# Router features taken from the unscaled residual and computed inside the output projection of a hybrid delta-net / attention / MoE layer

## What is computed

```python
x = x + merged @ w_out                        # output projection and residual
h = rms_norm(x, norm_ffn_w)                   # x / sqrt(mean(x^2) + eps) * norm_ffn_w
grp_prob  = softmax(h @ w_router_group + b_router_group)        # 4 groups
exp_logits = h @ w_router_expert + b_router_expert              # 16 experts
# best group, the best two experts in it, their weights; each chosen expert:
#   silu(h @ w_gate) * (h @ w_up) @ w_down, weighted and added to x
return rms_norm(x, norm_final_w)
```

## Time and profile before

| | |
|---|---|
| median of 3 runs | 768.96 us (768.24 to 773.33) |
| profiled execution, own time | 771.36 us |
| its span | 769.6 us |
| PE busy | 674.8 us (88%) |
| DVE / ACT / POOL busy | 62% / 50% / 22% |
| mean granted PE clock | 0.926 |

### The profile page before, as it was taken

The page is one execution under the profiler, slowest core; times in us unless marked ns, Lnnn a source line. Parts: engine busy times, 40 slices in busy tenths (PEclk is TensorE's granted clock), DMA queues, the critical chain, the costliest instruction groups (busy, mean ns, idle before and its releaser), DMA issues.

```text
span 769.6 us, 9253 instructions
## 1 busy us (share of the span) xinstructions
PE 674.8 (88%) x3386; PEld 557.1 (72%) x3388; DVE 479.9 (62%) x789; ACT 383.1 (50%) x647; POOL 169.5 (22%) x216
## 2 busy tenths in 40 slices
PE   5998796968989999999698999989999999999820
PEld 4677675746768888888587788658878888888710
DVE  5686646455452233444267265579989999999527
ACT  7366532523342243323343125237888988998612
POOL 6000000069700000000000000014555555555200
PEclk9999997978798999999899998689999999999965
DMA  8513311240032211112213735056877877977144
GB/s 263 183 56 62 58 45 56 69 137 1 5 84 85 61 55 56 55 55 94 72 55 110 282 155 199 22 157 192 282 220 232 287 241 249 317 252 254 39 153 191
DMA packets 73712, 104.62 MB, mean 136 GB/s; under 512 B 31625, under 2 KB 53186, under 8 KB 73538
## 3 DMA queue, kind: packets, MB, share of 16 engines
q1 hardware_dynamic: 60912, 95.57, 38.4%
q0 software_dynamic: 12672, 8.43, 3.6%
q10 hardware_dynamic: 82, 0.03, 0.0%
HBM read 123.89 MB, written 17.83 MB: 184 GB/s over the span
## 4 chain that ended last, share of the span: by engine, by line
PE 78%; DVE 9%; ACT 6%; issue 4%; DMA 3%; SPq 1%; DVEq 0%; ACTq 0%; POOLq 0%
PE bank L1510 20%; PE bank L1512 19%; PE bank L1511 19%; PE bank L1894 2%; PE bank L1639 2%; PE bank L1853 2%; PE bank L1837 2%; DMA w_raw<-in_w_in 1%; ACT w_hi L706 1%; ACT square_kq_T L740 1%; PE bank L1670 1%; PE bank L1657 1%; DMA expert_rows<-expert_rows_hbm 1%; DVE down_lo L1294 1%; PE bank L1669 1%
## 5 line engine op out<-in xcount | busy, mean ns | idle before, releaser
L1510 PE MATMUL bank<-h_hi,w_hi 128*128 128x512 f32 x304 | 125.3, 412 | 3.3 <-DVE h_lo L995 2.4
L1511 PE MATMUL bank<-h_lo,w_hi 128*128 128x512 f32 x304 | 120.3, 396 | 0.0
L1512 PE MATMUL bank<-h_hi,w_lo 128*128 128x512 f32 x304 | 120.2, 395 | 0.0
L1294 DVE TENSOR_TENSOR gate_up_lo<-ew_raw,gate_up_hi 128x1024 fp32r<-128x1024 f32 x92 | 108.3, 1220 | 6.0 <-ACT gate_up_hi L901 3.6
L653 POOL DMA_INDIRECT unit_tokens<-ffn_rows,row_index x23 | 30.8, 1338 | 320.3 <-DVE row_index L1416 304.7
L978 DVE TENSOR_TENSOR w_lo<-w_raw,w_hi 128x2048 fp32r<-128x2048 f32 x26 | 59.8, 2299 | 64.2 <-ACT w_hi L706 64.2
L901 ACT ACTIVATE gate_up_hi<-ew_raw 128x1024 fp32r<-128x1024 f32 x92 | 92.1, 1056 | 9.9 <-DMA ew_raw<-in_w_gate,extra_weight_rows 8.3
L1510 PE MATMUL bank<-gate_up_hi,unit_in_hi 128*128 128x512 f32 x184 | 75.8, 412 | 0.0
L1512 PE MATMUL bank<-gate_up_hi,unit_in_lo 128*128 128x512 f32 x184 | 72.2, 392 | 0.0
L1511 PE MATMUL bank<-gate_up_lo,unit_in_hi 128*128 128x512 f32 x184 | 71.8, 390 | 0.0
L1510 PEld LDWEIGHTS bank<-h_hi,w_hi 128*128 128x128 f32 x304 | 58.5, 192 | 14.8 <-DVE w_lo L990 2.6
(11 more groups left out here) (353 smaller groups left out, 1334.4 us busy)
## 6 DMA issues: line engine op xcount, KB each, us to landing
w_raw<-in_w_in SPq DMA_DIRECT2D x17, 1024.0 KB, 5.2
ew_raw<-in_w_gate SPq DMA_DIRECT2D x32, 512.0 KB
ew_raw<-in_w_up SPq DMA_DIRECT2D x32, 512.0 KB
ew_raw<-in_w_down SPq DMA_DIRECT2D x32, 512.0 KB
w_raw<-in_w_out SPq DMA_DIRECT2D x4, 1024.0 KB, 5.1
expert_rows<-expert_rows_hbm SPq DMA_DIRECT2D x8, 512.0 KB, 6.6
x_T<-in_x SPq DMA_DIRECT2D x4, 512.0 KB, 5.3
w_raw<-in_w_in SPq DMA_DIRECT2D x8, 256.0 KB, 4.3
```

The source lines that it names most:

```text
L1294: dve.tensor_tensor(dst, eraw[slot][:, :], hi.bitcast(F32), ALU.subtract).then_inc(elo_done, 1)
L1510: pe.matmul(out_ap, lhs_hi, rhs_hi, start=first, stop=False)
L1511: pe.matmul(out_ap, lhs_hi, rhs_lo, start=False, stop=False)
L1512: return pe.matmul(out_ap, lhs_lo, rhs_hi, start=False, stop=last)
```

## The change

The router no longer reads the normed tokens. PE transposes the residual y itself, in natural feature order, 4 blocks at a time: `residual_turn(0, t)` after each tile of the third quarter of the output projection, `residual_logits(0, t)`, `residual_turn(1, t - 1)` and `residual_logits(1, t - 2)` after the tiles of the fourth. What is left over follows the projection. The turns go round banks 4, 5 and 6, all logits are summed in bank 7. ACT copies the first halves of all tiles, DVE the second halves. norm_ffn_w is loaded as 8 more columns of `small_cols` and multiplied into the router weights once; the two router weight loads move in SP's queue from the start to the side projection, with another layout. DVE multiplies the logits by the norm's factor while adding the bias (4 instructions for 1). ACT's square sums come after its four copies and write to another scratch place. `ffn_norm(3)` moves behind the choice of experts on DVE. The fill matmuls are as before.

```diff
-        rows = at("small_rows", [57, P], F32, r_tmp + 4096)
+        rows = at("small_rows", [65, P], F32, r_tmp + 4096)
-        hf = at("ffn_in_F", [P, KT, S], F32, r_h + 16384)
+        hf = [at(f"residual_F{i}", [P, 4, S], F32, o) for i, o in enumerate((r_o, r_b + 8192))]
+        junk_m = at("square_junk_ffn", [P, D], F32, ffn_raw + 8192)
...
+                if u == U_SIDE + 4:
+                    sp.dma_start(rw_raw[:, :, 0:NG], a["w_router_group"][0].rearrange("(k p) n -> p k n", k=KT)).then_inc(x2_in, 16)
+                    sp.dma_start(rw_raw[:, :, NG:], a["w_router_expert"][0].rearrange("(k p) n -> p k n", k=KT)).then_inc(x2_in, 16)
-                    sp.dma_start(rw_raw[:, :, 0:NG], a["w_router_group"][0].rearrange("(p k) n -> p k n", k=KT)).then_inc(small_in, 16)
-                    sp.dma_start(rw_raw[:, :, NG:], a["w_router_expert"][0].rearrange("(p k) n -> p k n", k=KT)).then_inc(small_in, 16)
...
+            act.dma_start(rows[57:65, :], a["norm_ffn_w"][0].rearrange("(k p) -> k p", p=P)).then_inc(rows_in, 16)
...
             for t in range(TT):
+                act.wait_ge(tt_ps, t + 1)
+                act.activation(hf[0][:, :, t * P:(t + 1) * P], bank4(4 + t % 3), ACT.Copy).then_inc(hf_act, 1)
+            act.wait_ge(lo_done, split_count(UNITS_PRE - 1))
+            for t in range(TT):
                 act.wait_ge(y_done, 4 + t + 1)
                 if t:
                     act.wait_ge(ssq2, t)
-                act.activation(junk[:, :], y[:, t, :], ACT.Square, accum_out=ssq[:, t:t + 1]).then_inc(ssq2, 1)
+                act.activation(junk_m[:, :], y[:, t, :], ACT.Square, accum_out=ssq[:, t:t + 1]).then_inc(ssq2, 1)
...
-            for t in range(TT):
-                act.wait_ge(tt_ps, t + 1)
-                act.activation(hf[:, 0:4, t * P:(t + 1) * P], bank4(4 + 2 * (t % 2)), ACT.Copy).then_inc(hf_act, 1)
...
-            dve.wait_ge(x2_in, 48)
+            dve.wait_ge(x2_in, 80)
+            dve.tensor_tensor(rw_raw[:, :, :], rw_raw[:, :, :], bc_last(cols[:, 57:65], NG + NE), ALU.mult)
...
+            def residual_features(t):
+
+                dve.wait_ge(tt_ps, TT + t + 1)
+                dve.tensor_copy(hf[1][:, :, t * P:(t + 1) * P], bank4(4 + (TT + t) % 3)).then_inc(hf_dve, 1)
 
             for t in range(TT):
                 residual(0, t)
             residual(1, 0)
-            residual(1, 1)
-            ffn_norm(0)
-            residual(1, 2)
-            ffn_norm(1)
-            residual(1, 3)
-            ffn_norm(2)
-            ffn_features(0)
-            ffn_norm(3)
             for t in range(1, TT):
-                ffn_features(t)
+                residual(1, t)
+                residual_features(t - 1)
+                if t < TT - 1:
+                    ffn_root(t - 1)
+                    ffn_norm(t - 1)
+            residual_features(TT - 1)
+            ffn_root(TT - 2)
+            ffn_norm(TT - 2)
+            ffn_root(TT - 1)
...
             dve.wait_ge(lg_ps, TT)
-            link(dve.tensor_tensor(lg[:, :, :], ps[0][:, 0:TT * (NG + NE)].rearrange("p (t c) -> p t c", t=TT),
-                                   bc_mid(brg[:, :], TT), ALU.add))
+            for t in range(TT):
+                ins = dve.scalar_tensor_tensor(lg[:, t, :], ps[7][:, (NG + NE) * t:(NG + NE) * (t + 1)], rst[:, t:t + 1],
+                                               brg[:, :], ALU.mult, ALU.add)
+            link(ins)
...
             sel_f = sel[:, :, :, :].rearrange("p t g e -> p (t g e)")
+            ffn_norm(TT - 1)
             dve.wait_ge(rank_ps, 1)
...
+            def residual_turn(half, t):
+
+                q = TT * half + t
+                pe.wait_ge(y_done, q + 1)
+                if 3 <= q < 3 + TT:
+                    pe.wait_ge(hf_act, q - 2)
+                elif q >= 3:
+                    pe.wait_ge(hf_dve, q - 2 - TT)
+                for k in range(4):
+                    c0 = P * (4 * half + k)
+                    ins = pe.transpose(bank4(4 + q % 3)[:, k, :], y[:, t, c0:c0 + P], ident[:, :])
+                ins.then_inc(tt_ps, 1)
+
+            def residual_logits(half, t):
+
+                if half:
+                    pe.wait_ge(hf_dve, t + 1)
+                else:
+                    pe.wait_ge(hf_act, t + 1)
+                    pe.wait_ge(y_done, TT)
+                n_c = NG + NE
+                for k in range(4):
+                    ins = pe.matmul(ps[7][:, n_c * t:n_c * (t + 1)], hf[half][:, k, t * P:(t + 1) * P], rw_raw[:, 4 * half + k, :],
+                                    start=half + t + k == 0, stop=half == 1 and t == TT - 1 and k == 3)
+                if half:
+                    ins.then_inc(lg_ps, 1)
+
             for n_ in range(2):
                 for kh in range(2):
...
                         if kh or t == TT - 1:
                             ins.then_inc(out_used, 1)
+                        if n_ and not kh:
+                            residual_turn(0, t)
+                        if n_ and kh:
+                            residual_logits(0, t)
+                            if t:
+                                residual_turn(1, t - 1)
+                            if t > 1:
+                                residual_logits(1, t - 2)
+            residual_turn(1, TT - 1)
+            residual_logits(1, TT - 2)
+            residual_logits(1, TT - 1)
```

More of the change, by code:

```diff
@@ L244, in build @@
                                    for q, n_ in enumerate(("score_max", "score_max_neg", "sink_term", "prob_sum", "prob_norm")))
-        cols = new("small_cols", [P, 57])
+        cols = new("small_cols", [P, 65])
         ssq = new("sum_squares", [P, TT])
@@ L725, in _ @@
             act.activation(kv_(whi[0])[:, :, P:], kv_(raw[0])[:, :, P:], ACT.Copy).then_inc(hi_done, 1)
-            act.wait_ge(small_in, 128)
+            act.wait_ge(small_in, 96)
             act.activation(ba_hi[:, :, :], ba_raw[:, :, :], ACT.Copy).then_inc(ba_hi_done, 1)
@@ L981, in _ @@
             dve.wait_ge(rows_ps, 1)
-            dve.tensor_copy(cols[:, :], ps[7][:, 0:57]).then_inc(cols_done, 1)
+            dve.tensor_copy(cols[:, :], ps[7][:, 0:65]).then_inc(cols_done, 1)
             for i in range(EG):
@@ L1317, in residual, with ffn_root, ffn_norm @@
                 dve.tensor_tensor(o, o, ps[4 * (1 - n_) + t][:, :], ALU.add).then_inc(y_done, 1)
-            def ffn_norm(t):
+            def ffn_root(t):
                 dve.wait_ge(rms_root, t + 1)
                 link(dve.reciprocal(rst[:, t:t + 1], rst[:, t:t + 1]))
+            def ffn_norm(t):
                 dve.scalar_tensor_tensor(tx[:, t, :], y[:, t, :], rst[:, t:t + 1], nffn[:, :],
                                          ALU.mult, ALU.mult).then_inc(t_scaled, 1)
-            def ffn_features(t):
-                dve.wait_ge(tt_ps, t + 1)
-                dve.tensor_copy(hf[:, 4:8, t * P:(t + 1) * P], bank4(5 + 2 * (t % 2))).then_inc(hf_dve, 1)
+            def residual_features(t):
+                dve.wait_ge(tt_ps, TT + t + 1)
+                dve.tensor_copy(hf[1][:, :, t * P:(t + 1) * P], bank4(4 + (TT + t) % 3)).then_inc(hf_dve, 1)
             for t in range(TT):
@@ L1514, in _ @@
             pe.wait_ge(ident_set, 1)
-            pe.wait_ge(rows_in, 48)
-            pe.transpose(ps[7][:, 0:57], rows[:, :], ident[0:57, 0:57]).then_inc(rows_ps, 1)
+            pe.wait_ge(rows_in, 64)
+            pe.transpose(ps[7][:, 0:65], rows[:, :], ident[0:65, 0:65]).then_inc(rows_ps, 1)
             for t in range(TT):
@@ L1818, in _ @@
                             ins.then_inc(out_used, 1)
-            def tile_turn(t):
-                pe.wait_ge(t_scaled, t + 1)
-                if t >= 2:
-                    pe.wait_ge(hf_act, t - 1)
-                    pe.wait_ge(hf_dve, t - 1)
-                for k in range(KT):
-                    ins = pe.transpose(bank4(4 + 2 * (t % 2) + k // 4)[:, k % 4, :],
-                                       tx[:, t, :].rearrange("p (c k) -> p k c", k=KT)[:, k, :], ident[:, :])
-                ins.then_inc(tt_ps, 1)
-            def tile_logits(t):
-                pe.wait_ge(hf_act, t + 1)
-                pe.wait_ge(hf_dve, t + 1)
-                n_c = NG + NE
-                for k in range(KT):
-                    ins = pe.matmul(ps[0][:, n_c * t:n_c * (t + 1)], hf[:, k, t * P:(t + 1) * P], rw_raw[:, k, :],
-                                    start=k == 0, stop=k == KT - 1)
-                ins.then_inc(lg_ps, 1)
-            pe.wait_ge(y_done, 5)
-            tile_turn(0)
-            tile_turn(1)
-            tile_logits(0)
-            tile_turn(2)
-            tile_turn(3)
-            for t in range(1, TT):
-                tile_logits(t)
+                        if n_ and not kh:
[9 more added lines that the diff above has]
+            residual_logits(1, TT - 1)
             def keep_busy(count):
```

## The result

The changed kernel takes 776.18 us (median of 8 runs, 775.03 to 778.28), the kernel before 770.41 (8 runs, 768.24 to 773.33), so the medians are 5.8 us apart (0.75%). The ratio is 1.0109, 95% interval 1.0073 to 1.0145, which would be +8.4 us (5.6 to 11.2). The forecast was 775.6, +6.6 over the median of 768.96 that the kernel before had in three runs. The profiled execution took 776.85 us, with a span of 775.1 (before: 771.36 and 769.6).

A forecast was written before the change was run, and what follows sets the result against it. Bound taken: PE's projection, then 17.4 us of small router matmuls before the logits. PE terms summed to 42.8 us; logits at 43.4 against 36.65, +6.7, less 0.1 behind, gave 775.6 us; range 772.0 to 781.5.

The forecast's parts named there:

- The stall: Third projection quarter: PE's first transposes wait for DVE's first residual add, 9.3 us, bounds 9.0 and 9.8.
- The clock: Behind PE's idle time: lower clock level for a while, costing 2.1 us, bounds 1.5 and 4.5.
- The router records: Router matmuls on PE, mostly between projection matmuls: 64 records at 0.121 us each, 7.7 us.
- The transposes: PE's turns of the residual: 32 transposes at 0.12 us each, 3.9 us.
- The changes back: Seven returns on PE from light to dense matmuls: 0.1 us each, 0.7 us in all.
- The end: Last turn ends at 490.9; DVE's copy, norm of tile 2 and reciprocals follow; logits read at 493.4.
- Behind the logits: From logits to rank: extra DVE instructions and the moved norm lie under PE's fill wait; -0.1 us taken.
- rival 3: First expert unit waits for a late gather instead of the fill: +1 to +3 us, 778.0; chance 0.15.
- The start: Program start: fourth load on ACT's queue adds under 0.4 us to 5.74 and disappears.
- rival 2: Clock stays low in the mixed light and dense part: 9.1 us more, 784.7; chance 0.10.
- rival 4: Clock kept up behind the projection, last fill run cheaper, stall's aftermath only 1.5: 773.3; chance 0.20.
- rival 5: No stall, all features come out under the projection: 11.4 us less, 764.2; chance 0.02.

The follow-up runs named there:

- the fourth load alone: The kernel before plus the fourth load of rows and the 65-row transpose, nothing else of the change: 768.82 us, ratio 1.0016.
- the adds first: Changed kernel with DVE's router-weight multiplication and four first-half residual adds moved ahead of the last weight's low part: 763.05 us, ratio 0.993.
- the turns late: Changed kernel with all four first-half turns moved behind the third quarter's last tile on PE, DVE's order kept: 766.29 us, ratio 0.9954.

## Why the prediction was right, step by step

*The stall* was 9.01 us against 9.3 forecast. It is what the change costs: put alone into the kernel before it gives +10.05 us to the logits, and taken out of the changed kernel in two ways, on DVE's side and on PE's, it gives 11.5 and 10.0. That two edits on different engines give nearly the same, and that the one on PE leaves DVE's queue as it is, speaks for PE meeting DVE too early, not for work that DVE hasn't time for. The multiplication of the router weights took 0.26 us (taken: 0.3) and one add some 0.6.

*The clock* after the stall was forecast at 2.1 us. By the rows it is 0.67 on four transposes (1.11 against 0.44) and 0.2 on each of ten dense matmuls, 2.7; the kernel in which PE is kept busy through the stall gives 2.0 to 2.25. Both lie within the bounds, 1.5 to 4.5.

*The router records* were the term that I sized wrong: 7.7 us for 64 at 0.121 each. The 48 ahead of the last turn's end took 0.80 for eight, 4.8 us, and the last 16 took 1.86 (487.55 to 489.41), 6.7 in all. The price was misread more than the kernel misjudged. The row of 1.93 us for 16 runs to the end of the last record, and a record lasts 0.27 us, but the next instruction begins before that end: in the timeline of the kernel before the transposes behind those 16 records start at 473.85, 1.78 us behind the first record.

```profile
472.07 1.93 PE L1837 MATMUL bank<-router_raw,ffn_in_F 128*128 128x20 f32 x16 [1.09 <-ACT ffn_in_F L915]
473.85 2.70 PE L1827 MATMUL bank<-ident,ffn_in_T 128*128 128x128 f32 x16
```

That is 0.11 from start to start, the same pace as in the changed kernel; a group of eight behind transposes is at 0.10 because its first record is followed by the second after only 0.03 us. *The transposes* took 0.43 to 0.48 for four, 3.6 us in all instead of 3.9, for the same reason (16 in 1.94, but 0.11 from start to start). *The changes back* to dense matmuls: the first one takes 0.32 instead of 0.23 in the chain, 0.09 each against 0.1.

*The end*: from the last turn's end at 487.73 to the logits 2.2 us, forecast 2.5; DVE with its copy, the norm of the third tile and a reciprocal is indeed later than PE. In sum, from the end of the first tile (447.87) to the logits it is 42.1 us, against 43.4 forecast and 36.65 before: -0.1 for the stall (9.16 from the end of the last matmul to the transposes), -0.3 for the end, +0.6 for the clock, -1.0 for the 48 router records ahead of the last turn, -0.3 for the transposes, and 0.2 that I can't place.

*Behind the logits* the rank is read 7.16 us later, without a wait, as forecast (at most 7.2). But the fill ahead of the first unit took 6.32 us for 16 where before it was 5.31 for 15, 5.55 with the first; the granted clock was 0.54 over it, before 0.63. The unit's transposes come 20.75 us behind the logits instead of 20.35. That is +0.4 where I had -0.1.

*The gather* (rival 3) is issued at 501.49, 11.6 us behind the logits, and was covered by the fill: the unit's transposes (L1912) follow the fill (L1871) in the chain above. The mechanism of the rival was there: it took 6.6 us to land, against 4.6 in the kernel with the fourth load alone, whose stores and loads are in the old order. But it landed at 508.1, 2.6 us ahead of the transposes. With 8 fill matmuls the gather is what ends the wait.

*The start* was the claim that failed. The fourth load was to add under 0.4 us and to disappear; it landed 1.9 us later (7.65 against 5.74), ACT's first product was 1.6 later, and at 158 us the program was still 1.1 behind (159.76 against 158.62). In the other kernels with this load the first matmul stands at 6.7 to 7.6 us and ACT's product at 17.9 to 18.5 (before: 17.9), so that most or all of it is absorbed; the profiled execution of the changed kernel was the worst of them, and not by the load alone. Its 32 transposes of x, all that PE does there, took longer than in the kernel with the adds first:

```profile
9.21 6.64 PE L1532 MATMUL bank<-ident,x_T 128*128 128x128 f32 x32 [1.21 <-DVE x_T L991]
8.73 5.41 PE L1531 MATMUL bank<-ident,x_T 128*128 128x128 f32 x32 [1.22 <-DVE x_T L991]
```

No times showed a cost: without the load 1.012, with it 1.0109. The size of the delay was wrong, and that it matters little to the time was right.

*The rivals.* The clock staying low in the mixed part (rival 2) is refuted by the windows from 463 to 485 us, at 1.00 with turns and router groups between the dense ones. The rule of the Trainium skill (TensorE: Matmul & The Clock Gate, Part 4: PE-mode transpose), that the full rate does not engage for transposes, does not carry over to transposes in groups of four between twelve dense matmuls: the trace does not agree on the level, which is 1.00, with 0.11 us from one transpose to the next. Nor does it hold here for transposes alone. At the start of the program PE runs nothing but one small matmul and 32 transposes; in the kernel before the first 15 follow each other 0.21 us apart, and the last eight 0.11 apart. These are the spacings that transposes have at 0.50 and at 1.00 behind the projection. The profile's row of the granted clock has 1.00 over both stretches, so that here the level is read from the spacing alone:

```profile
7.27 3.46 PE L1522 MATMUL bank<-ident,x_T 128*128 128x128 f32 x15 [1.21 <-DVE x_T L988]
```

The clock kept behind the projection (rival 4) did not come either: 0.97 up to 490 us and 0.50 right behind, and the last fill run became dearer instead of cheaper. No stall (rival 5) is what the kernel with the adds first has; it was priced at 764.2 us, and took 763.05.

*What I had not in the sum* are the shifts outside the part that the change touches, -1.9 us before the out-projection and +1.8 behind the first unit. They nearly cancel in the profiled execution. Over the runs they are part of the spread; that the median came out within 0.6 us of the forecast is in part luck, since the first and the last term of the span were not forecast at all, and since the median of the kernel before rose by 1.45 us from three runs to eight, which hides 0.8 us of a difference forecast at 6.6 and measured at 5.8. What sets where these stretches at 0.50 fall stays open.

## What to carry to other kernels

Putting light work between dense matmuls can keep the clock up (1.00 from 463 to 485 us, where 11.6 us of the same work in one piece were at 0.50) and take a tail away, but each step moved forward on one engine has to be held against the queue of the engine that feeds it: here four adds stood 9 us too late on an engine that nobody waited for before. The same change brings the logits 6.3 us forward with the adds moved and 5.2 us back without. When two engines' orders don't fit, either side can be moved, and the side with the least behind it (the adds first, 1.4 us better than the turns late in the time to the logits) is the one to try first.

A fill run that looks like dead time on the chain is not worth its mean price. Halving one moved the first unit 1.7 us forward and the time not at all: the eight matmuls that stayed were at the lower level, and so was what came behind them.

The price of one instruction in a run is the distance from start to start. The busy time of a merged row has the last one's whole length in it: 16 records read as 0.121 us each were 0.11.

## What the runs showed of the hardware that I had not expected

A small fourth load in a row of small loads on one queue moved the landing that PE waits for by 1.0 to 1.9 us against the kernel before (6.69 to 7.65 us in six kernels; 5.58 to 5.78 in the four with three loads), where under 0.4 had been taken.

Transposes with no dense matmul around them went over to the spacing of the upper level by themselves, from 0.21 to 0.11 us apart in the course of the program's first 32. The change came after 17 of them in the kernel before, and after 29 in the changed one.

The level of the clock far from an edit changes from kernel to kernel: 0.79 instead of 1.00 over 8 us behind the first unit, in the changed kernel and in the ones with the turns late and with PE kept busy, but not in the one with the adds first, at the same instructions. It costs some 1.8 us, and a single profile can't be read for a change of that size.
